# Second-table sums kept in six PSUM banks; half of tile 0's gathered rows summed by VectorE

## What is computed

```
u2 = modulate(x, sh2, sc2)                       # 512 x 1024
e_idx, gates = top-16 of 16384 per head (8 heads)  # 128 experts for each token
a   = einsum('thkd,td->thk', u_tab[e_idx], u2)   # first table
wgt = gelu(a) * gates
y_p = einsum('thk,thkd->td', wgt, v_tab[e_idx])  # second table
x   = layer_norm(ALPHA * x + (1 + g2) * y_p, ln2_g, ln2_b)
```

## Time and profile before

| | us |
|---|---|
| median of 3 runs | 1704.18 |
| lowest and highest | 1703.92 and 1704.64 |
| span of the profiled execution, first to last instruction | 1705.5 |
| PE busy | 1623.8 |
| DVE busy | 1313.6 |
| ACT busy | 689.8 |
| POOL busy | 651.7 |

### The profile page before, as it was taken

The page is one execution under the profiler, slowest core; times in us unless marked ns, Lnnn a source line. Parts: engine busy times, 40 slices in busy tenths (PEclk is TensorE's granted clock), DMA queues, the critical chain, the costliest instruction groups (busy, mean ns, idle before and its releaser), DMA issues.

```text
span 1705.5 us, 23213 instructions
## 1 busy us (share of the span) xinstructions
PE 1623.8 (95%) x8286; PEld 1373.1 (81%) x8286; DVE 1313.6 (77%) x2712; ACT 689.8 (40%) x1037; POOL 651.7 (38%) x450
## 2 busy tenths in 40 slices
PE   5999999994999999999997999999989999999996
PEld 3887777773899999999997998998966677676775
DVE  5489776888589799989957898998965555556588
ACT  4335565425334354545543343333233333333332
POOL 0210000002125778677745754743804432332211
PEclk9999999997999999999998999999999999999998
DMA  8223224452776657576789988988969999999962
GB/s 347 99 80 119 87 99 173 148 198 93 248 256 195 160 173 192 150 222 171 201 245 361 391 314 312 402 323 313 347 228 381 403 363 356 343 383 358 363 227 81
DMA packets 180898, 422.29 MB, mean 248 GB/s; under 512 B 33584, under 2 KB 66480, under 8 KB 180528
## 3 DMA queue, kind: packets, MB, share of 16 engines
q1 hardware_dynamic: 90688, 264.44, 43.0%
q0 software_dynamic: 57200, 139.58, 23.9%
q10 hardware_dynamic: 32896, 16.78, 3.6%
HBM read 375.55 MB, written 45.15 MB: 247 GB/s over the span
## 4 chain that ended last, share of the span: by engine, by line
PE 72%; DVE 20%; DMA 4%; issue 2%; ACT 2%; SPq 0%; POOL 0%; DVEq 0%; ACTq 0%; POOLq 0%
PE bank L1766 21%; PE bank L1767 21%; PE bank L1768 21%; PE bank L2098 3%; DVE one L1554 2%; DVE wlo L1386 2%; DVE one L1552 2%; DVE one L1556 2%; DMA gates_by_key<-stage 1%; DMA gring<-gates_by_key 1%; PE bank L1912 1%; PE bank L1897 1%; PE bank L2047 1%; PE bank L2023 1%; DVE stats L1042 1%
## 5 line engine op out<-in xcount | busy, mean ns | idle before, releaser
L1766 PE MATMUL bank<-act_hi,whi 128*128 128x384 f32 (+1 forms) x1352 | 482.2, 357 | 12.8 <-ACT gelz L907 4.9
L1767 PE MATMUL bank<-act_lo,whi 128*128 128x384 f32 (+1 forms) x1352 | 473.0, 350 | 0.0
L1768 PE MATMUL bank<-act_hi,wlo 128*128 128x384 f32 (+1 forms) x1352 | 472.9, 350 | 0.0
L1766 PE MATMUL bank<-vhi,eh 128*128 128x512 f32 x768 | 306.0, 398 | 8.6 <-DVE vlo L1594 8.6
L1767 PE MATMUL bank<-vlo,eh 128*128 128x512 f32 x768 | 302.5, 394 | 0.0
L1768 PE MATMUL bank<-vhi,el 128*128 128x512 f32 x768 | 301.4, 392 | 0.0
L1766 PEld LDWEIGHTS bank<-act_hi,whi 128*128 128x128 f32 x1352 | 255.8, 189 | 31.2 <-issue 8.3
L1594 DVE TENSOR_TENSOR vlo<-vraw,vhi 128x512 fp32r<-128x512 f32 x256 | 176.5, 698 | 133.1 <-ACT vhi L960 121.4
L1767 PEld LDWEIGHTS bank<-act_lo,whi 128*128 128x128 f32 x1352 | 255.9, 189 | 13.9
L1768 PEld LDWEIGHTS bank<-act_hi,wlo 128*128 128x128 f32 x1352 | 255.4, 189 | 13.2
L696 POOL DMA_INDIRECT gates_by_key<-selW,selS x128 | 234.0, 1828 | 70.1 <-issue 45.3
(11 more groups left out here) (247 smaller groups left out, 1995.1 us busy)
## 6 DMA issues: line engine op xcount, KB each, us to landing
raw<-in_u_t_dram SPq DMA_DIRECT2D x128, 512.0 KB
vraw<-in_v_tab_dram SPq DMA_DIRECT2D x256, 256.0 KB
raw<-in_wblk_dram SPq DMA_DIRECT2D x61, 512.0 KB, 4.2
gring<-gates_by_key SPq DMA_DIRECT2D x32, 768.0 KB
raw<-in_w_modt_dram SPq DMA_DIRECT2D x32, 512.0 KB, 3.3
gates_by_key<-stage ACTq DMA_DIRECT2D x8, 2048.0 KB
gelu_ahead<-gelz SPq DMA_DIRECT2D x20, 768.0 KB
gback<-gelu_ahead SPq DMA_DIRECT2D x40, 384.0 KB
```

Of the source, the lines that this page charges most:

```text
L1766: mm(o, wh, mh, start=start, stop=False)
L1767: mm(o, wh, ml, start=False, stop=False)
L1768: return mm(o, wl, mh, start=False, stop=stop)
```

## The change

Four edits, all in the second sub-layer:

1. **Dense sums stay in PSUM.** `pv_bank` gives banks 2 to 4 to half 0 and 5 to 7 to half 1 for all groups; the matmuls start at group 0 and stop at group 15. `add`, `residual` and `gated_tiles` are gone; DVE reads the banks once, in group 15.
2. **Half of the second rows by DVE.** Of the 128 picks of each token of tile 0, the first 64 (`OWN_ROWS`) are gathered with tokens on partitions: one gather brings one row for each of the 128 tokens, into a ring of three slots (`acc[:, 0:3]`, `OWN_RING`). DVE multiplies it by the token's weight and adds it to `acc[:, 3]` (`own_row`, 64 operations of 128x1024), after `low_v` in the first six or seven steps of half 0 of groups 5 to 14 (`ROWS_OF`).
3. **Paired tokens.** The other 64 picks go the old way, but two tokens share a gather (64 rows each) and the columns of `wz`. 64 gathers and 16 quads remain, at k = 5 of half 0 and, where `QUADS_OF` says 2, of half 1, into banks 0 and 1. POOL issues the gathers alternately: row n, then pair n. Row n waits until DVE has used row n - 3 (`own_v`); pair n waits for its ring slot as before.
4. **Moved.** `diagonals` and `gate_row` go from group 12 to group 5 (PE after product k = 2); `own_sum` joins both parts in group 15.

```diff
+OWN_ROWS = SLOTS // 2
+OWN_RING = TT - 1
+PAIRS_OF = P // 2
+IN_STRIP = QUAD // 2
+QUADS = PAIRS_OF // 4
+QUADS_OF = (2, 1, 2, 1, 2, 1, 2, 2, 2, 1)
+ROWS_OF = (6, 7, 6, 7, 6, 7, 6, 6, 6, 7)
...
-        def pv_bank(g, half, t):
-            if half == 0:
-                return bank[2 + t]
-            return bank[(5, 6, 7)[t] if g < V_GROUP else (0, 1, 5)[t]]
+        def pv_bank(half, t):
+            return bank[2 + TD * half + t]
...
-            for n in range(P):
-                tok = n % 4 * QUAD + n // 4
+            def own_row(j):
+                need(pool, own_v, j - OWN_RING + 1)
+                pool.indirect_dma_start(
+                    out=acc[:, j % OWN_RING, :], out_offset=None, in_=v_tab,
+                    in_offset=bass.IndirectOffsetOnAxis(ap=idxN[:, j:j + 1], axis=0)).then_inc(vo_in[j % OWN_RING], 16)
+            for n in range(PAIRS_OF):
+                pair = n % 4 * IN_STRIP + n // 4
+                own_row(n)
                 if n < RING:
                     pool.wait_ge(dot_r, SLOTS - RING + n + 1)
                 else:
                     pool.wait_ge(quad_mm, (n - RING) // 4 + 1)
...
+            def own_row():
+                j = next(own_next)
+                dve.wait_ge(vo_in[j % OWN_RING], 16 * (j // OWN_RING + 1))
+                if j == 0:
+                    nc.vector.tensor_scalar(acc[:, TD, :], acc[:, 0, :], own_a[:, 0:1], None, ALU.mult).then_inc(own_v, 1)
+                else:
+                    dve.wait_ge(own_v, j)
+                    nc.vector.scalar_tensor_tensor(out=acc[:, TD, :], in0=acc[:, j % OWN_RING, :],
+                                                   scalar=own_a[:, j:j + 1], in1=acc[:, TD, :],
+                                                   op0=ALU.mult, op1=ALU.add).then_inc(own_v, 1)
...
+                    elif g - V_GROUP < len(ROWS_OF) and k < ROWS_OF[g - V_GROUP]:
+                        own_row()
...
                 for t in range(TD):
-                    if k == 0:
-                        need(pe, pv_add, 2 * TD * (g - 1) + TD * half + t + 1)
...
-                if 0 <= r and (k in (3, 7) if half == 0 or four else k == 4):
+                if 0 <= r < len(QUADS_OF) and k == 5 and half < QUADS_OF[r]:
+                    quad(sum(QUADS_OF[:r]) + half)
```

More of the change, by code:

```diff
@@ L93 @@
 QUAD = 32
+OWN_ROWS = SLOTS // 2
[5 more added lines that the diff above has]
+ROWS_OF = (6, 7, 6, 7, 6, 7, 6, 6, 6, 7)
+assert sum(QUADS_OF) == QUADS and sum(ROWS_OF) == OWN_ROWS
 ORDER = (1, 2, 3, 0)
@@ L362, in build @@
         wz_r = sem("wz_r")
-        vg_in = [sem(f"vg_in{i}") for i in range(RING)]
+        vo_in = [sem(f"vo_in{i}") for i in range(OWN_RING)]
+        own_v = sem("own_v")
         quad_mm = sem("quad_mm")
@@ L1615, in residual @@
-            def residual(t, half):
-                cut = slice(half * HALF, (half + 1) * HALF)
[L1618 to L1623, removed]
-                cut = slice(half * HALF, (half + 1) * HALF)
-                wait_sum(g, half, t)
-                nc.vector.tensor_tensor(acc[:, t, cut], pv_bank(g, half, t)[:, :], rows2[:, 0, cut],
-                                        ALU.mult).then_inc(pv_add, 1)
@@ L1630, in gated_sum @@
-            def gated_sum(g, t, half):
-                cut = slice(half * HALF, (half + 1) * HALF)
-                dve.wait_ge(pv_add, 2 * TD * g + TD * half + t + 1)
-                return nc.vector.tensor_tensor(xfin[:, t, cut], xfin[:, t, cut], acc[:, t, cut], ALU.add)
-            def gated_tiles(g, half):
-                for t in range(TD):
-                    gated(g, t, half)
-                for t in range(TD):
-                    last = gated_sum(g, t, half)
-                link(last)
@@ new lines, in last_sum @@
+            def last_sum(t, half):
+                cut = slice(half * HALF, (half + 1) * HALF)
+                dve.wait_ge(pv_add, TD * half + t + 1)
+                link(nc.vector.scalar_tensor_tensor(out=xfin[:, t, cut], in0=xfin[:, t, cut], scalar=ALPHA,
+                                                    in1=acc[:, t, cut], op0=ALU.mult, op1=ALU.add))
+                return bn(xfin, t, half)
+            own_next = iter(range(OWN_ROWS))
+            def own_row():
[8 more added lines that the diff above has]
+                                                   op0=ALU.mult, op1=ALU.add).then_inc(own_v, 1)
@@ L1655, in own_rows, with group @@
                 return bn(xfin, TD, half)
-            def group(g, first=False, last=False):
+            def group(g, last=False):
                 for k in range(GR):
                     if k == 0:
-                        if last:
-                            gated_tiles(g - 1, 1)
-                        elif first is not True:
-                            add(g - 1, 1, first == "second")
-                        if first is not True:
+                        if g > 0:
                             low_w(g, GR - 2)
@@ L2077, in second_product @@
                 pe.wait_ge(w_lo, GR * g + k + 1)
+                ends = g == NG - 1 and k == GR - 1
                 for t in range(TD):
-                    if k == 0:
-                        need(pe, pv_add, 2 * TD * (g - 1) + TD * half + t + 1)
                     c = slice(t * P, (t + 1) * P)
-                    last = three(pv_bank(g, half, t)[:, :], eh[:, k, c], el[:, k, c], vhi[:, n % VR, :], vlo[:, n % VR, :],
-                                 k == 0, k == GR - 1)
-                    if k == GR - 1 and t < TD - 1:
+                    last = three(pv_bank(half, t)[:, :], eh[:, k, c], el[:, k, c], vhi[:, n % VR, :], vlo[:, n % VR, :],
+                                 g == 0 and k == 0, ends)
+                    if ends and t < TD - 1:
                         last.then_inc(pv_mm, 1)
```

131 lines of the change are left out of this document (62 added, 69 removed).

## The result

| | before | changed |
|---|---|---|
| median, us | 1704.41 | 1723.48 |
| lowest and highest of four runs, us | 1703.92 to 1705.90 | 1721.98 to 1725.33 |
| span of the profiled execution, us | 1705.5 | 1720.2 |

The ratio is 1.0106 with a 95% interval of 1.0093 to 1.0119. The changed kernel is **slower** by 1.1%; forecast were 1696 us and a range that ended at 1718.

What follows compares the result with a forecast made beforehand. TensorE was taken as the bound, DMA transfers a near second. From 1705.5 us, a gain of 37.6 and a loss of 30 (waits 21.8, half clock 5.2, late rows 3) give 1697.9, so a median of 1696; range 1672 to 1718.

Steps and rivals of the forecast that it cites:

- 4.1 + 2.1 + 2.1 n: Groups 5 to 14: us from group start until n gathers landed; quad due at 12.3, waits sum to 21.8 us.
- so only the last matters: Late row operations, fourth to seventh of a group: TensorE has about 4.8 us in hand, only the seventh, 5 late, counts.
- The bound and the gain: TensorE sets each group's end; sixteen quads fewer give 33.0 us, group 4 to 5 and gate row 4.6, together 37.6.
- The mechanism and its places: Pair gathers stand behind row gathers waiting for DVE; TensorE waits before half 0's quad in groups 6, 8, 13 and 14.
- The first row operation ends 4.1 us after the group's start: DVE at a group's head: `vlo` starts without the add, first row operation ends 4.1 us after the start.
- POOL's own pace isn't the limit: POOL issues a gather in 0.94 + 0.30 us, or 1.49 + 0.30 beside DVE, against 2.1 us per gather moved.
- Half clock: TensorE returns at half clock after the two long quad waits, groups 6 and 14: 2.6 us each, 5.2 in all.
- Late rows and late loads: Late row operations in groups 5 to 14 and the load of `xfin` in group 12: 3 us lost.
- (C): Rival, chance 0.20: late rows hold DVE and so `vlo`, at 2.54 us per gather; waits 31.5, loss 50, time 1716 us.
- (B): Rival, chance 0.22: gathers land in time, 1.3 us each if q1 has little to move at a group's start; 1672 us.
- (D): Rival, chance 0.13: total DMA rate falls to about 370 GB/s, groups 5 to 14 take 388 us; 1701 to 1707.
- the sum stays: If DVE locks POOL out, later gathers are issued every 1.8 us, still under 2.1, leaving the 21.8 us of waits.

Runs made afterwards that it cites:

- experiment 3: Changed kernel with 61 of 64 row gathers left out, DVE reusing the same three rows (tile 0's sum not formed): 1668.99 us.
- experiment 4: Kernel before with dense sums kept in PSUM and the gate row in group 5; 32 quads, no rows on DVE: 1701.75 us.
- experiment 1: Changed kernel with only POOL's order altered: after the first eight, pair gathers follow, four at a time, the quad that frees their slots: 1682.65 us.
- experiment 2: Changed kernel with the quad of groups that have only one moved from half 0 to half 1: 1700.32 us.
- experiment 12: Changed kernel with five slots for gathered rows instead of three, same order of all instructions: 1682.07 us.
- experiment 8: experiment 1 with DVE's half 1 weights staggered from group 5, rows spread over a group's sixteen steps and pair gathers one a step: 1674.34 us.
- experiment 5: Changed kernel with row operations dealt like quads, 8 to groups with two quads and 4 to groups with one: 1717.84 us.
- experiment 9: Changed kernel with 61 of 64 row gathers fetching 256 bytes a row instead of 4096: 1701.04 us.

## Where the prediction was right, and which steps failed

The prediction failed at the price of the waits, "4.1 + 2.1 + 2.1 n", and at "so only the last matters" for the late rows. What it takes from TensorE, the mechanism and the places were right.

**The bound and the gain: right.** 32.8 us for 16 quads fewer (33.0 forecast, experiments 3 and 4). For the sums in PSUM with the moved gate row 3.8 us (experiment 4), and with the 1.1 us of the smaller `wz`, which experiment 4 doesn't have, 4.9 (4.6 forecast).

**The mechanism and its places: right.** POOL waits for DVE instead of quads. Of the groups named, all four wait, and the only other one is group 10, for 0.9 us, in which the count has one pair missing (group 5 has one too, and doesn't wait). Experiments 1, 2 and 12 each take the mechanism away in another manner, and the waits go.

**Its size: mis-sized, 31.6 us against 21.8.** Two terms of the sum failed.

- *The first row operation ends 4.1 us after the group's start.* It was 4.5, and 7.1 in group 6. In group 6 DVE comes out of half 1 behind TensorE: each step takes it 2.27 us, with 0.59 us of waiting for ACT in it, against 2.05 for a product. I had taken the head of group 9 of before, where DVE was on time. This is 4.2 us over the four groups.
- *n gathers land 2.1 + 2.1 n us later.* Measured from the end of the first row operation: 8.6 us for one missing pair (two gathers), 13.1 and 12.0 for two, 14.8 for three, 19.2 for four. That is about 5.2 + 1.75 n. For three and four pairs the forecast and the measurement agree within 0.4 us, for few pairs the fixed part decides: groups 8 and 13 wait 5.3 and 4.3 where 2.3 stood. I took the fixed part from a single gather that found the queue empty. In the group's head the last gather lands 5.4 to 6.8 us after its issue has ended. And "POOL's own pace isn't the limit" was false: beside DVE's operations its issues start up to 1.8 us apart (1.24 without), and in group 8 four issues take 7.2 us and the landing 5.9, which is the whole of the 13.1.

**Half clock: in four groups, not two.** I had put it behind waits longer than 4.93 us, as in the earlier trace rows. In the changed kernel it came behind every wait at a quad from 4.3 us on and not behind 0.9. On the quads alone it costs 4 * 1.72 = 6.9 us. Up to five matmuls behind each quad are slow as well, 3.2 us in all, so it is 10.1 us against 5.2; per quad 2.5 us, as forecast (2.6).

**Late rows and late loads: 10 us against 3.** "TensorE has about 4.8 us in hand, so only the last matters" failed. Rows arrive late from the fourth of a group on; DVE waited 33 times for one. TensorE stopped for `vlo` in groups 7, 9, 11 and 12 too, where no quad waited. Of the 9.8 us, 6.5 stand behind late rows. This is rival (C)'s mechanism, at the forecast's speed of gathers. Experiment 12 agrees: its longer ring takes away 5.8 us. The other 3.3 us are no rows: the two stops at the head of group 12 come before its first row operation (1545.75), behind a late `vraw` and a late load of gates. ACT, DVE and PE of the changed kernel:

```profile
1533.04 0.63 ACT L976 ACTIVATE vhi<-vraw 128x512 fp32r<-128x512 f32 x1 [4.20 <-DMA vraw<-in_v_tab_dram]
1537.31 0.56 DVE L1610 TENSOR_TENSOR wf<-gback,gring 128x384 f32<-128x384 f32 x1 [2.91 <-DMA gring<-gates_by_key]
1539.72 0.50 PE L1774 MATMUL bank<-vhi,eh 128*128 128x512 f32 x1 [1.78 <-DVE vlo L1622]
1545.88 0.50 PE L1774 MATMUL bank<-vhi,eh 128*128 128x512 f32 x1 [1.55 <-DVE vlo L1622]
```

SP had issued the loads of `xfin` and `rows` (3.1 MB) between 1509.8 and 1512.3. That they made these two late is likely, but no experiment tests it.

**The end** from the start of the last matmul is 12.4 us and was 10.5; this term was missing, and the experiments have one or the other (10.9 in experiment 8, 12.5 in experiment 1). I did not follow it.

The span lies 1720.2 - 1697.9 = 22.3 us above the sum. The terms give 9.8 for the waits, 4.9 for half clock, 7.2 for late rows and loads and 1.9 for the end, together 23.8; the 1.5 us too many are not assigned.

**The rivals.** (B) at 1672 is what the change gives when the gathers are in time: 1674.3 in experiment 8. But (B) wanted that from free engines alone. They were not full at the heads of groups 8 and 14, and the gathers still took 1.75 us each and 5.2 us on top. (C)'s sum of waits, 31.5 us, is the measured one by luck: a gather took 1.75 us and not 2.54. (D) fell: the DMA carried 354 GB/s on average from 1262 to 1650 in the changed kernel and 387 from 1262 to 1602 in experiment 8, with the same gathers and loads; at the heads of groups the engines were short of requests, not the requests short of engines. Its price was wrong too: 388 us for the phase against TensorE's 363 take 25 us from the gain, which is 1692 and not 1701 to 1707. The 358 GB/s that the Trainium skill gives as a limit (DMA: Bandwidth & Descriptors, Specifications) do not bind here: 404 GB/s over 26 us in experiment 1. POOL's slower issues, put aside since "the sum stays", did matter. The Trainium skill, DMA: Bandwidth & Descriptors, SWDGE vs HWDGE vs iDMA, says that GpSimd writes descriptors into SBUF state from which VectorE locks it out during its 2-port perf mode. The trace agrees in that issues start 1.8 us apart beside row operations and 1.24 apart without. That this lock is the cause isn't shown: no run tells the mode of a row operation, and it takes 1.28 us, where the first one, which has one source (L1650), takes 0.75 for the same 128x1024. The Trainium skill, Perfetto Trace Analysis, DMA Instruction — SWDGE (GPSIMD), says that such a row ends when the descriptors are made, not when the data has moved; the rows agree, with 4.3 to 6.8 us between the two.

**What I should have asked.** The chain was known, and the sum of its parts stood 8 us from no gain at all. Nearly every error had one direction, since I took each duration from a place where nothing else was in the way.

## What to carry to other kernels

An in-order queue that serves two consumers couples them: put each request behind the event that frees its own slot, never behind a slot of the other. Before a change that takes work from the bound engine, count for every stage how many requests are still unissued when it begins, and price each with rows from a loaded stretch, the fixed part too. Here a ring two slots longer was worth as much as the right order (1682 us both), and spreading the requests over the stage as well gave more than either (1674).

## What was unexpected in the hardware

- The length of an idle time alone doesn't tell whether TensorE comes back at half clock. In experiment 5 quads took 3.59 and 3.58 us after 2.28 and 2.40 us of idle time (groups 7 and 8), and 1.92 after 2.61 and 2.92 (groups 9 and 10).
- q0 and q1 do not always share packet for packet. In experiment 9, from 1622 to 1629, with pair gathers outstanding, q1 moved 562 packets and q0 279.
- With a sixteenth of a row's bytes a row gather costs POOL the same time: 0.95 us alone and 1.5 beside DVE.
